# First norm and lead stage of a two-block forward pass: warming products, low-rank columns in four column groups, and product slabs ahead of the modulation slabs

## The reference, cut to what matters

```python
h = rmsnorm(x, norm_mix)                       # 256 tokens x 1024
proj = h @ w_in                                # split: keys, queries, values, ... of both branches, gates
qa, ka, va, ra, a_lr, qb, kb, vb, gates = jnp.split(proj, points, axis=-1)
log_a = jax.nn.log_sigmoid(a_lr @ w_lr_up + b_forget) / GLA_TAU     # a_lr: 16 columns
mod = silu(c) @ ada_w[0] + ada_b[0]            # modulation of the second block, for c and c_ctx
```

## Time and profile before

| | before |
|---|---|
| median of 3 runs | 1426.61 us (1423.76 to 1427.33) |
| profiled execution | 1430.85 us, its span 1429.1 us |
| PE busy in the span | 1380.7 us, 97% |
| DVE, ACT, POOL busy | 980.2, 820.4, 573.4 us |
| mean granted TensorE clock | 0.991 |

### The profile page before, as it was taken

The page is one execution under the profiler, slowest core; times in us unless marked ns, Lnnn a source line. Parts: engine busy times, 40 slices in busy tenths (PEclk is TensorE's granted clock), DMA queues, the critical chain, the costliest instruction groups (busy, mean ns, idle before and its releaser), DMA issues.

```text
span 1429.1 us, 27586 instructions
## 1 busy us (share of the span) xinstructions
PE 1380.7 (97%) x10866; PEld 1288.9 (90%) x10866; DVE 980.2 (69%) x1302; ACT 820.4 (57%) x1178; POOL 573.4 (40%) x190
## 2 busy tenths in 40 slices
PE   7999999999999999999999998999999888999997
PEld 4778889999999998899999998999998758899997
DVE  3312684847899987679999887665666783766665
ACT  3532565645788836657888365545544574555543
POOL 2343436455233313452222234655653201465662
PEclk9999999999999999999999999999999999999999
DMA  8675775455344444773444436655546401555540
GB/s 315 244 290 195 264 265 192 155 199 191 119 177 176 177 177 168 275 282 132 177 176 177 177 148 237 250 219 211 191 158 241 173 30 60 206 179 188 188 179 30
DMA packets 39430, 271.01 MB, mean 190 GB/s; under 512 B 4596, under 2 KB 5876, under 8 KB 6958
## 3 DMA queue, kind: packets, MB, share of 16 engines
q1 hardware_dynamic: 39342, 269.76, 50.8%
HBM read 268.68 MB, written 1.06 MB: 189 GB/s over the span
## 4 chain that ended last, share of the span: by engine, by line
PE 82%; DVE 5%; ACT 5%; DMA 4%; POOL 1%; issue 1%; SPq 0%; DVEq 0%; ACTq 0%
PE ps L1834 21%; PE ps L1835 21%; PE ps L1836 21%; PE ps L630 9%; DMA raw<-w_dram 4%; PE ps L1980 2%; ACT whi L808 2%; POOL wlo L766 1%; PE ps L2343 1%; PE ps L1871 1%; DVE wlo L1249 1%; PE ps L2331 1%; ACT mqk L889 1%; ACT bufA L1171 1%; PE ps L1943 1%
## 5 line engine op out<-in xcount | busy, mean ns | idle before, releaser
L766 POOL TENSOR_TENSOR wlo<-raw,whi 128x1024 fp32r<-128x1024 f32 (+1 forms) x181 | 571.2, 3159 | 831.4 <-ACT whi L808 831.2
L808 ACT ACTIVATE whi<-raw 128x2048 fp32r<-128x2048 f32 x181 | 345.6, 1911 | 412.0 <-PE ps L1836 224.5
L1249 DVE TENSOR_TENSOR wlo<-raw,whi 128x1024 fp32r<-128x1024 f32 (+1 forms) x181 | 280.4, 1550 | 310.1 <-ACT whi L808 308.7
L1834 PE MATMUL ps<-h_hi,whi 128*128 128x256 f32 x1232 | 353.7, 287 | 1.0 <-POOL wlo L766 0.9
L1835 PE MATMUL ps<-h_lo,whi 128*128 128x256 f32 x1232 | 348.4, 283 | 0.0
L1836 PE MATMUL ps<-h_hi,wlo 128*128 128x256 f32 x1232 | 348.3, 283 | 0.0
L1834 PE MATMUL ps<-g_hi,whi 128*128 128x256 f32 x1040 | 297.8, 286 | 6.4 <-POOL wlo L766 3.1
L1835 PE MATMUL ps<-g_lo,whi 128*128 128x256 f32 x1040 | 294.2, 283 | 0.0
L1836 PE MATMUL ps<-g_hi,wlo 128*128 128x256 f32 x1040 | 294.2, 283 | 0.0
L1834 PEld LDWEIGHTS ps<-h_hi,whi 128*128 128x128 f32 x1232 | 236.0, 192 | 9.1 <-issue 7.7
L1835 PEld LDWEIGHTS ps<-h_lo,whi 128*128 128x128 f32 x1232 | 236.2, 192 | 0.4
(11 more groups left out here) (283 smaller groups left out, 1891.9 us busy)
## 6 DMA issues: line engine op xcount, KB each, us to landing
raw<-w_dram SPq DMA_DIRECT2D x245, 1024.0 KB, 4.9
brev<-w_dram SPq DMA_DIRECT2D x2, 1024.0 KB, 7.2
gates<-w_dram SPq DMA_DIRECT2D x2, 1024.0 KB, 8.5
xlat<-xT_dram SPq DMA_DIRECT2D x2, 512.0 KB, 4.5
brev<-w_first_keys_dram SPq DMA_DIRECT2D x1, 1024.0 KB, 9.3
brev<-bias_rows SPq DMA_DIRECT2D x1, 1024.0 KB, 9.3
brev<-ctxT_dram SPq DMA_DIRECT2D x1, 1024.0 KB, 7.4
sra<-w_dram SPq DMA_DIRECT2D x1, 1024.0 KB, 8.1
```

The costliest lines, as they stand in the source:

```text
L766: pool.tensor_tensor(wlo[:, g.slot, part], raw[:, g.slot, part], whi[:, g.slot, part].bitcast(F32), ALU.subtract).then_inc(lo2_done, 1)
L808: act.activation(whi[:, g.slot, :], raw[:, g.slot, :], ACT.Copy).then_inc(hi_done, 1)
L1249: dve.tensor_tensor(wlo[:, g.slot, part], raw[:, g.slot, part], whi[:, g.slot, part].bitcast(F32), ALU.subtract)\
L1834: pe.matmul(out, w[0], x[0], start=start, stop=False, skip_group_check=True)
```

## The change

- **Warming.** PE starts with 12 fp32 products of `ones` by `ones` (128 columns) into an unused bank, before the means.
- **Low rank and first keys together.** For each normed tile k as it is scaled, PE makes one low-rank product and the two key products of that tile. The low-rank weights are padded to 32 columns, product k goes to column group k mod 4, so the 8 products leave four partial sums in 128 rows of bank 6; `w_lr_up` is stored four times over (128 rows) so that the gate product adds them. The constant row comes from a bias column instead of a memset.
- **Head loads.** The bias table's two loads and the first keys are issued before the first slab; the low-rank up weights (now 256 KB) and `sel` come after it. The low-rank down weights grow from 64 to 128 KB.
- **Order of slabs.** The four modulation slabs ahead of m2 go behind it, and after m4, m8, m10 and m12 there are two modulation slabs in a row instead of one. From a15 on LEAD is the same, from m14 on STREAM is:

```diff
+WARMING = 12
-ADA_FIRST = 3
-LEAD = [("ada", i) for i in range(ADA_FIRST)]
+TWO_ADA = (4, 8, 10, 12)
+LEAD = []
 for _g in range(2, N_MIX):
-    if _g + 1 < N_ADA:
-        LEAD.append(("ada", _g + 1))
     LEAD.append(("mix", _g))
+    for _ in range(2 if _g in TWO_ADA else 1):
+        if len(LEAD) - _g + 1 < N_ADA:
+            LEAD.append(("ada", len(LEAD) - _g + 1))
...
 def lead_stream():
-    out, rest = LEAD[:ADA_FIRST], LEAD[ADA_FIRST:]
-    while rest:
-        if rest[0][0] == "ada":
-            out += [rest[1], rest[0]]
-            rest = rest[2:]
+    out, held = [], []
+    for item in LEAD:
+        if item[0] == "ada":
+            held.append(item)
         else:
-            out.append(rest.pop(0))
-    return out
+            out += [item, *held]
+            held = []
+    return out + held
...
-        lr_down = mqk[:, 0, 0, 0:KT * RANK].rearrange("p (k n) -> p k n", k=KT)
+        lr_down = mqk[:, 0, 0, 0:KT * QUAD].rearrange("p (k n) -> p k n", k=KT)
...
+            sp.dma_start(relb[0:BUCKETS, :], io["rel_bias"]).then_inc(s_small, 16)
+            sp.dma_start(sra[0:BUCKETS + 1, 0:2, :], io["onehot"]).then_inc(s_small, 16)
+            sp.dma_start(first_keys, io["w_first_keys"]).then_inc(s_keys, 16)
...
             split_hi(0, bufA, h_hi)
+            for n in range(RING):
+                hi(Slab(n))
+            act.wait_ge(s_cols, 16)
             act.wait_ge(lr_done, 1)
-            act.activation(alr[0:RANK, :], ps[0:RANK, 6, 0:T], ACT.Copy).then_inc(mix_drained, 1)
+            act.activation(alr, ps[:, 6, 0:T], ACT.Identity, bias=col("lr_one")).then_inc(mix_drained, 1)
...
             scale_split(0, xlat, lambda t: col("norm_mix", t), 0, bufA, H, None)
+            lo(Slab(0))
             dve.wait_ge(s_cols, 16)
...
+            for _ in range(WARMING):
+                pe.matmul(ps[:, 7, 0:P], ones[:, :], ones[:, :], start=True, stop=True)
...
+            for k in range(KT):
+                pe.wait_ge(y_done, k + 1)
+                y = bufA[:, k * T:k * T + T]
+                r = QUAD * (k % 4)
+                ins = pe.matmul(ps[r:r + QUAD, 6, 0:T], lr_down[:, k, :], y, start=(k < 4), stop=(k >= 4), skip_group_check=True)
+                if k == KT - 1:
+                    ins.then_inc(lr_done, 1)
+                for m in range(2):
+                    ins = pe.matmul(ps[:, 0, m * T:m * T + T], w[:, k, m * P:m * P + P], y, start=(k == 0 and m == 0),
+                                    stop=(k == KT - 1), skip_group_check=True)
+            ins.then_inc(keys_done, 1)
```

More of the change, by code:

```diff
@@ L950, in _, with drain @@
             split_hi(0, bufA, h_hi)
+            for n in range(RING):
+                hi(Slab(n))
+            act.wait_ge(s_cols, 16)
             act.wait_ge(lr_done, 1)
-            act.activation(alr[0:RANK, :], ps[0:RANK, 6, 0:T], ACT.Copy).then_inc(mix_drained, 1)
[L953 to L958, removed]
+            act.activation(alr, ps[:, 6, 0:T], ACT.Identity, bias=col("lr_one")).then_inc(mix_drained, 1)
+            act.wait_ge(keys_done, 1)
+            act.activation(ka[:, 0:2, :], ps[:, 0, :], ACT.Copy).then_inc(mix_drained, 1)
+            def drain(g, out, func=ACT.Copy, scale=1.0):
+                act.activation(out, ps[:, mix_bank(g), :], func, scale=scale).then_inc(mix_drained, 1)
             def drain_wide(out):
@@ L987, in _ @@
                 elif g < 11:
-                    drain(n, mqk[:, 1, 2 * (g - 9):2 * (g - 9) + 2, :])
+                    drain(g, mqk[:, 1, 2 * (g - 9):2 * (g - 9) + 2, :])
                 elif g < 13:
                     out = mqk[:, 0, 2 * (g - 11):2 * (g - 11) + 2, :].rearrange("p t (b x) -> p t b x", b=2)
-                    act.activation(backwards(out), ps[:, mix_bank(n), :].rearrange("p (t b x) -> p t b x", t=2, b=2), ACT.Copy,
+                    act.activation(backwards(out), ps[:, mix_bank(g), :].rearrange("p (t b x) -> p t b x", t=2, b=2), ACT.Copy,
                                    scale=DH ** -0.5).then_inc(mix_drained, 1)
@@ L998, in _ @@
                         act.wait_ge(tab_done, 1)
-                    drain(n, sra[:, 2 * (g - 15):2 * (g - 15) + 2, :], ACT.Silu)
+                    drain(g, sra[:, 2 * (g - 15):2 * (g - 15) + 2, :], ACT.Silu)
                 else:
@@ L1002, in _ @@
                         act.wait_ge(o_done, 1)
-                    drain(n, gates[:, 2 * (g - 19):2 * (g - 19) + 2, :], ACT.Sigmoid)
+                    drain(g, gates[:, 2 * (g - 19):2 * (g - 19) + 2, :], ACT.Sigmoid)
                 if g == 2:
@@ L2013, in _ @@
             ins.then_inc(ms_done, 1)
[L2014 to L2032 removed]
+            pe.wait_ge(s_relb, 1)
+            pe.wait_ge(s_small, 32)
+            pe.matmul(ps[0:H_MOBA, 5, :], relb[:, :], sra[0:BUCKETS + 1, 0:2, :], start=True, stop=True).then_inc(tab_done, 1)
+            pe.wait_ge(s_lr, 16)
+            pe.wait_ge(s_keys, 16)
+            w = first_keys.rearrange("p (k n) -> p k n", k=KT)
+            for k in range(KT):
[9 more added lines that the diff above has]
+            ins.then_inc(keys_done, 1)
+            pe.wait_ge(cond_f, 2)
             for n, (kind, g) in enumerate(LEAD):
@@ L2040, in _ @@
                 else:
-                    if n >= 4 and LEAD[n - 4][0] == "mix":
-                        pe.wait_ge(mix_drained, LEAD[n - 4][1] + 1)
-                    elif mix_bank(n) % 2:
-                        pe.wait_ge(mod_done, N_ADA // MOST - mix_bank(n) // 2)
+                    if mix_bank(g) % 2:
+                        pe.wait_ge(mod_done, N_ADA // MOST - mix_bank(g) // 2)
+                    elif g > 2:
+                        pe.wait_ge(mix_drained, max(k for k in range(1, g) if mix_bank(k) == mix_bank(g)) + 1)
                     if 5 <= g < 9 or 13 <= g < 15:
@@ L2184, in _ @@
             for i in range(4):
-                last = max(n for n in range(len(LEAD)) if mix_bank(n) == i)
-                pe.wait_ge(mix_drained, LEAD[last][1] + 1)
+                pe.wait_ge(mix_drained, max(g for g in range(N_MIX) if mix_bank(g) == i) + 1)
                 features(Slab(BASE["gla"] + i), i, G)
@@ L2414 @@
     o_kb, o_vb, o_g = o_qb + MOBA_W, o_qb + 2 * MOBA_W, o_qb + 3 * MOBA_W
-    lr = win[:, o_lr:o_lr + RANK].reshape(KT, P, RANK).transpose(1, 0, 2)
+    lr = np.zeros((P, KT, QUAD), np.float32)
+    lr[:, :, 0:RANK] = win[:, o_lr:o_lr + RANK].reshape(KT, P, RANK).transpose(1, 0, 2)
+    lr_up = np.zeros((P, GLA_W), np.float32)
+    for r in range(0, P, QUAD):
+        lr_up[r:r + RANK] = a["w_lr_up"][0]
+    lr_up[RANK] = a["b_forget"][0]
     first_keys = win[:, o_ka:o_ka + SLABC].reshape(KT, P, SLABC).transpose(1, 0, 2).reshape(P, SLAB)
```

52 lines of the change are left out of this document (18 added, 34 removed).

## The result

| | before | after |
|---|---|---|
| median | 1425.06 us (5 runs, 1423.74 to 1427.33) | 1452.57 us (5 runs, 1449.78 to 1457.95) |
| ratio | | 1.0184, 95% interval 1.0164 to 1.0203 |
| profiled execution | 1430.85 us, span 1429.1 | 1457.95 us, span 1456.2 |
| mean granted TensorE clock | 0.991 | 0.983 |
| root of the second norm (a point behind the lead stage) | 254.47 us | 277.20 us |

The changed kernel is 27.5 us slower. Forecast were 22.2 us more and 1448.8 us, in a range of 1436 to 1456. On the page PE is busy 1396.4 us (before 1380.7).

What follows compares the result with a forecast made beforehand. PE, busy in 97% of the span, was taken as the bound. Head, gaps, m7 and clock terms up to m14 summed to +22.2 us, taking the median from 1426.61 to 1448.8 us, 8-in-10 range 1436 to 1456.

Steps and rivals of the forecast that it cites:

- The mechanism: Neighbouring product slabs three places apart: the split waits until PE has used the slab before, at m6, m10, m12, m14.
- head: Start to m2: warming gains 1.1 us, the loop of low-rank and key products ends so that m2 starts at 26.6.
- gap before m6: PE idle 4.5 us: a split chain of 5.5 us after m5's last product, less a4's 1.0.
- m6 to m7 (11.6): m8's later landing and split delay ACT's drain of m6; m7 starts 11.6 us after m6, before 10.1: +1.5.
- low clock on m7: m7 no longer follows the gap in which the clock fell: -2.5 us.
- gap before m10: PE idle 4.5 us, as only a9 stands between m9 and m10.
- low clock on m10: The clock falls in the idle time before m10: 2.5 us, between 0 and 3.5.
- around m12, clock included: m11 to m12: 4.3 us idle in two pieces as three queues meet, plus 1.5 us of low clock.
- gap before m14: PE idle 4.5 us, as only a15 stands between m13 and m14.
- 2.4 + 0.35 + 1.9 + 1.7 + 1.2 + 0.1: m11 to m12: ACT wait, turn, second state product, DVE's parts, handover; m12 starts 7.6 us after m11.
- The rival built on it: Head: low-rank products overlap in four column groups at 1.0 us, m2 starts 5.1 us sooner, 1443.7 us; chance 0.08.
- The clock rival: The gaps come, but m10, m12, m14 and the head run at full clock: +14.4, 1441.0 us; chance 0.13.

Runs made afterwards that it cites:

- second trace of the kernel before: The kernel before, unedited, profiled a second time: 1425.68 us, span 1424.0.
- the second pair: The changed kernel and the kernel before, both unedited and run again: 1453.27 us (ratio 1.0177) and 1425.68 us.
- the kernel before with the drain first: The kernel before with one edit, ACT drains m6 before it splits m8: 1426.96 us, ratio 0.9995 against the kernel before.
- the gaps taken away: The changed kernel with m6, m10, m12 and m14 left unsplit (their results wrong by content): 1427.72 us, ratio 1.0001 against the kernel before.
- low-rank block: The changed kernel with the 8 low-rank products in one block behind the keys, in four column groups: 1449.07 us, ratio 1.0141 against the kernel before.
- groups of three: The changed kernel with three modulation slabs in a row behind m11 and m13, single ones elsewhere: 1427.92 us, ratio 1.0008 against the kernel before.
- drain first: The changed kernel with both three-slab groups and low-rank products behind the keys, ACT draining m6 before splitting m8: 1420.30 us, ratio 0.9955 against the kernel before.

## Why the prediction was right, and where its sizes were off

The mechanism, its four places and its sign were right. Term by term, in the first traces of both kernels:

| step of the sum | forecast | measured | from |
|---|---|---|---|
| head (m2 at 26.6) | -1.1 | -0.8 | m2 at 26.97; 31.73 - 26.97 - 4.0 |
| gap before m6 | +4.5 | +4.6 | 4.61 |
| m6 to m7 (11.6) | +1.5 | +1.1 | 63.62 to 74.80, 11.2, against 10.1 |
| low clock on m7 | -2.5 | -1.1 | 74.80 to 81.95, 7.15, against 8.23 |
| gap before m10 | +4.5 | +4.6 | 4.62 |
| low clock on m10 | +2.5 | +1.5 | 105.21 to 112.61, 7.4, against 5.9 |
| around m12, clock included | +5.8 | +7.7 | m11's end 122.4 to m12 131.37, 9.0 less 3.3 of work; m12 to 139.32, 8.0 against 5.9 |
| gap before m14 | +4.5 | +4.6 | 4.62 |
| low clock on m14 | +2.5 | +2.5 | 161.53 to 169.64, 8.1, against 5.6 |
| sum | +22.2 | +24.7 | |

Read directly, m14 ends 24.3 us later. At the root of the second norm it is 277.20 - 254.47 = 22.7 us. The 1.6 us between are one wait: PE stood 2.06 us for DVE before line 2149 in the kernel before and stands 0.48 there in the changed one (at 225.70), so part of the delay was absorbed, which I did not allow for. So against the profiled execution on which it was built, the lead stage came out within 0.5 us, and that is luck: small errors cancel. m7's low clock was taken as gone and was there (1.4 us), the stretch around m12 was 1.9 us too small, m10's clock term 1.0 too large, and the 1.6 were absorbed. Around m12 the step "2.4 + 0.35 + 1.9 + 1.7 + 1.2 + 0.1" counted the second state product at the full clock; after the first idle piece of 2.33 us it ran at the lower level and took 3.14 us instead of 1.99. The head met its term by two errors as well: DVE began the normed tiles at 12.18, as forecast (12.1), but PE began only at 12.81, when the first tile was done, a step that I had left out; and the loop took 14.2 us where 14.5 were forecast with its low clock.

**Why the time rose by 27.5 us and not 22.** The term that was mis-sized most is m7, "+1.5 ... -2.5". Both halves set the new kernel against one trace in which m6 to m7 took 10.1 us and m7 ran at a low clock. In the second trace of the kernel before the distance is 7.4 us (m6 starts behind a7 at 62.4, m7 at 69.85) and the clock is up. Against that the term is 11.2 - 7.4 = +3.8 for the wait, and 7.15 - 5.71 = +1.4 for the clock: +5.2 instead of -1.0. With it the sum would have been 28.4, and the traces of the second pair are 28.1 us apart in span (1452.1 and 1424.0), 29.6 at the root, and the medians of their runs 26.7. Two smaller terms hang on the trace in the same way: the head, which gains 0.8 us in the first pair, loses 0.3 in the second (m2 at 30.81 and 27.14, less 4.0), and the kernel before then waits 0.89 us before m9, which the changed one does not. I had noted that the profiled execution was 4.2 us above the median, and then carried it over as a constant of both kernels. It was no constant: a part of it was this wait, and the change replaces it. That this accounts for the medians rests on two traces of either kernel and one of the kernel before with the drain first; the waits of the executions that were not profiled are not known.

The rule of the Trainium skill on tiling modes (a change of mode drains the engine, "TensorEngine Tiling (Array Packing)", Key Properties) held here in kind: in the loop, one there-and-back costs 1.61 - 6 x 0.224 = 0.27 us, forecast was 0.3; by the 8 of them 2.1 us. Its table of speedups holds for the block (16 records in 1.07 us, where one by one at 0.224 they are 3.6) and not for the interleaved form. The rival built on it (chance 0.08) was wrong for this change and right as a variant: m2 starts 5.4 us sooner (5.2 at the root). 4.4 us of that are the arrangement and 1.6 the clock in the loop, less 0.6 in which m2 waits for its split.

The clock rival (0.13) is out: PEclk is at 0.50 to 0.70 behind every gap, and keeping PE busy brought back 5.6 us at m10, m12 and m14, where I had 6.5 in the forecast. The rival that the split wait is covered (0.07) is out, too; even with the gaps taken away the order only reached the time of the kernel before, not 1419.6, which rested on the same unlucky wait before m7.

The first pair of traces drew apart by another 4.4 us behind the second norm (27.1 us in span against 22.7 at the root). 3.9 of it are waits that only the changed kernel's first trace has: PE waits 6.2 us there for POOL's lower parts and 2.8 for landings, where the kernel before waits 4.0 and 1.1, and the second pair 4.3 and 1.1 (changed), 4.3 and 1.3 (before). So they belong to that execution, which was also the slowest of its five, and not to the change.

Not settled: what makes a slab of 1 MB land after 4.8 us in one execution and 7.5 in the next, with the same issue order; and what decides whether the clock falls in the loop of the head.

## What to carry to other kernels

In a ring, a buffer that is filled from the landed one (here the split parts) has a wait of its own: count the distance in places between two neighbours that need it, and avoid that it equals the ring's depth; two or four places apart there was no such wait, three cost a whole split chain of 5.6 us less the 1.0 us of work between. The small-column products here paid in a block of their own and not between full-width ones. Before a term is set against a wait in the profile that was ended by a landing, look whether the profiled execution is slower than the median, and read the wait in a second profile of the same kernel.

## What the runs showed that I had not expected

- One and the same wait behind a landing was 0.64 us in one execution of the kernel before and 3.35 in another, and with the low clock behind it this was 5.2 of the 6.6 us by which the two traces differ at the root (247.89 and 254.47).
- The length of an idle time did not decide by itself whether the clock fell behind it. Behind 2.33 us it fell in the changed kernel (PEclk 0.60 from 125 to 130 us) and behind 2.06 us it did not in the kernel before; but behind the 2.01 us before the loop of the head it fell in some traces and not in others, with the same instructions ahead.
- The clock in the head went with how long the 12 warming products took. In the traces where they took 4.5 us (low-rank block, groups of three, drain first) the keys behind ran at the full level from the start; in those where they took 4.9 to 5.5 us (the other seven) the clock was low for their first 3 to 6 us, which costs 1.6 to 2.8 us. Why, the runs do not show; no kernel was profiled often enough to say how frequent either is.
- 12 products of ones, 5.49 us long and free of cost, brought the means from 3.68 us (3.75 in the changed kernel without them) to two pairs of 1.13 us.
